# Row products behind the first squares, a split taken out of the junction chains, and deferred lows and bonus products in mixer 2, in a two-block transformer kernel on one Trainium2 core

## The reference, cut to what matters

```
for i in 0, 1:
    x += 0.5 * rms(swiglu(rms(x)))         # FFN "i0", width 2816
    x += rms(mixer_i(rms(x)))              # mixer 0: GLA and gated delta rule; mixer 1 ("mixer 2"): RWKV-7 and LRU
    x += 0.5 * rms(swiglu(rms(x)))         # FFN "i1"
```

## Time and profile before

| | us |
|---|---|
| median of 3 runs | 2829.31 (2826.69 to 2831.57) |
| profiled execution, its own time | 2830.72 |
| its span, first to last instruction | 2828.7 |
| PE busy | 2680.0 (95%) |
| weight loads / DVE / ACT busy | 2134.7 / 1558.9 / 1032.8 |
| mean granted clock of TensorE | 0.97 |

### The profile page before, as it was taken

How to read it: one execution, slowest core, us unless ns; L and a number is a source line. 1 busy time by engine, 2 the same in 40 slices (tenths; PEclk the granted TensorE clock), 3 DMA queues, 4 the chain that set the end, 5 groups by cost and what they waited for, 6 DMA issues and landing times.

```text
span 2828.7 us, 37623 instructions
## 1 busy us (share of the span) xinstructions
PE 2680.0 (95%) x15612; PEld 2134.7 (75%) x15612; DVE 1558.9 (55%) x2235; ACT 1032.8 (37%) x1536; POOL 18.8 (1%) x39
## 2 busy tenths in 40 slices
PE   7999799989999999999999999999999898999997
PEld 4766575668888788787888887888876687788886
DVE  6875867585244663634643446424465866553344
ACT  3354536442223354224422234222346422432222
POOL 0100000000000000000000000000000000000000
PEclk9999999999999997999999999999999999999998
DMA  8611231122332320112223232233222200232322
GB/s 313 233 54 64 88 115 57 55 75 88 105 98 79 100 75 30 39 31 67 90 86 108 89 98 86 89 101 102 78 90 69 65 4 3 82 97 84 110 78 72
DMA packets 71448, 243.90 MB, mean 86 GB/s; under 512 B 7920, under 2 KB 8176, under 8 KB 70256
## 3 DMA queue, kind: packets, MB, share of 16 engines
q1 hardware_dynamic: 66240, 222.11, 24.5%
q0 software_dynamic: 5040, 19.40, 1.9%
HBM read 239.38 MB, written 2.10 MB: 85 GB/s over the span
## 4 chain that ended last, share of the span: by engine, by line
PE 86%; DVE 7%; ACT 3%; issue 2%; DMA 1%; SPq 0%; DVEq 0%; ACTq 0%
PE bank L418 84%; ACT work L1471 1%; DVE work L2120 1%; DMA work<-w_ada 1%; PE bank L624 1%; DVE weights_low L2137 1%; ACT weights_high L1537 1%; DVE residual L2120 1%; DVE work L2314 1%; DVE work L2337 1%; DVE rstd L2127 0%; ACT silu_gate L1471 0%; ACT L1471 0%; ACT normed L1471 0%; DMA residual<-x_in 0%
## 5 line engine op out<-in xcount | busy, mean ns | idle before, releaser
L418 PE MATMUL bank<-normed,weights_high 128*128 128x512 f32 x4848 | 1543.0, 400 | 36.8 <-ACT normed L1471 36.8
L418 PEld LDWEIGHTS bank<-normed,weights_high 128*128 128x128 f32 x4848 | 914.8, 191 | 265.7 <-issue 80.1
L418 PE MATMUL bank<-normed,weights_low 128*128 128x512 f32 x2424 | 955.8, 394 | 0.0
L1537 ACT ACTIVATE weights_high<-ring 128x1024 fp32r<-128x1024 f32 (+2 forms) x431 | 420.7, 979 | 881.9 <-PE bank L418 881.8
L2137 DVE TENSOR_TENSOR weights_low<-ring,weights_high 128x1024 fp32r<-128x1024 f32 (+2 forms) x431 | 484.0, 1125 | 433.0 <-ACT weights_high L1537 429.5
L418 PEld LDWEIGHTS bank<-normed,weights_low 128*128 128x128 f32 x2424 | 461.8, 191 | 97.8
L418 PE MATMUL bank<-hidden,weights_high 128*128 128x512 f32 x1408 | 433.4, 389 | 0.0
L418 PEld LDWEIGHTS bank<-hidden,weights_high 128*128 128x128 f32 x1408 | 264.3, 188 | 54.8
L2510 DVE TENSOR_TENSOR silu_gate<-bank,rstd 128x512 f32<-128x512 f32 x176 | 120.8, 690 | 325.1 <-PE bank L418 325.0
L418 PE MATMUL bank<-hidden,weights_low 128*128 128x512 f32 x704 | 273.9, 389 | 0.0
L418 PE MATMUL bank<-work 64*64 64x64 f32 (+6 forms) x1600 | 146.0, 315 | 11.6 <-DVE work L2987 6.1
(11 more groups left out here) (263 smaller groups left out, 1934.3 us busy)
## 6 DMA issues: line engine op xcount, KB each, us to landing
ring<-w_k SPq DMA_DIRECT2D x303, 512.0 KB, 3.5
ring<-w_d SPq DMA_DIRECT2D x64, 384.0 KB, 3.0
ring<-w_d SPq DMA_DIRECT2D x64, 320.0 KB, 2.8
work<-w_ada POOLq DMA_DIRECT2D x32, 512.0 KB, 6.6
work<-w_shift SPq DMA_DIRECT2D x4, 1024.0 KB, 13.4
work<-w_ada SPq DMA_DIRECT2D x7, 512.0 KB, 19.1
constants<-cst_in SPq DMA_DIRECT2D x1, 2176.0 KB, 19.9
residual<-x_in SPq DMA_DIRECT2D x4, 512.0 KB, 6.2
```

What stands on the lines that cost most here:

```text
L418: return pe.matmul(o, lhsT, rhs, start=start, stop=stop, skip_group_check=True)
L1537: nc.scalar.activation(WH[:, u % SPLIT, 0:w], RING[:, u % SLOTS, 0:w], ACT.Copy).then_inc(unit_high, 1)
```

## The change

On PE, `shift_rows(0)` moves behind ms, to rows 1 to 3. At the FFN junctions `high` and `low` of the fourth next unit go behind the last output tile: `high` just ahead of the root, `low` between the reciprocal and the wait for the spread. At the mixout junctions only `low` moves, to the same place. In mixer 2 the lows of mixout's units 0 to 3 move from units 18 to 21 of the projection to the four steps of `rwkv`; bonus products move behind units 20 and 21; ly's third and fourth tile get buffers of their own (two of the running decay sums' tiles, free once `rkb` 3 is done), squares alternate between two buffers, and copies 20 and 21 no longer wait for `lru_out`. ACT makes an empty Sigmoid after unit 4's copy (`RSTD[:, 0, 8:9]`).

```diff
+        def gelu_input(i):
+            return (raw(U_LY), raw(U_LY + 1), cst("sel"), tile(12))[i]
+        def gelu_square(i):
+            return (STATE[:], tile(23))[i % 2]
@@ PE: layer_norm, odd_projection, program
                     step(mm(PS[6][:], cst("onesD"), tile(0)), "mean", norm)
-                    shift_rows(0)
-                    elif j in (19, 20):
-                        bonus(2 * j - 38)
-                        bonus(2 * j - 37)
+                    elif j in (20, 21):
+                        bonus(2 * j - 40)
+                        bonus(2 * j - 39)
-                    for i in range(1, 4):
+                    for i in range(4):
                         shift_rows(i)
@@ ACT: ffn
                         high(down + 2 * t + SPLIT)
-                        high(down + 2 * t + 1 + SPLIT)
+                        if q == 0 or t < KT - 1:
+                            high(down + 2 * t + 1 + SPLIT)
...
+                high(down + 2 * KT - 1 + SPLIT)
                 root(("post", f))
@@ ACT: odd_projection
-                        act.wait_ge(*(dve_done("gelu0", i - 1) if i else dve_done("kgated", 3)))
-                        a(STATE[:], raw(j), ACT.Square, "gelu0", i, ...)
-                        if i:
-                            gelu_gate(i - 1)
-                        else:
+                        act.wait_ge(*(dve_done("kgated", 3), dve_done("rkb", 1), dve_done("gelu0", 0), dve_done("gelu0", 1))[i])
+                        a(gelu_square(i), gelu_input(i), ACT.Square, "gelu0", i, ...)
+                        if i >= 2:
+                            gelu_gate(i - 2)
+                        elif i == 0:
...
+                    if j == U_WA:
+                        a(RSTD[:, 0, 8:9], v("one"), ACT.Sigmoid)
...
+                gelu_gate(2)
                 gelu_gate(3)
@@ DVE: post_norm, ffn
                 reciprocal_std(("post", name))
+                low(last_low)
                 dve.wait_ge(*pe_done("spread", ("post", name)))
...
                         low(down + 2 * t + SPLIT)
-                        low(down + 2 * t + 1 + SPLIT)
+                        if q == 0 or t < KT - 1:
+                            low(down + 2 * t + 1 + SPLIT)
@@ DVE: odd_projection
                     if j >= U_LY + 2:
-                        lru_out(j - 2 - U_LY)
-                        dve.wait_ge(*dve_done("ylru", j - 2 - U_LY))
+                        dve.wait_ge(*dve_done("rkb", 3))
...
-                    if j > LEAD:
+                    if LEAD < j < N_ODD - SPLIT:
                         low(u0 + j + SPLIT)
...
-                    elif j >= 19:
-                        if j == 19:
-                            queries_decayed(2)
-                            queries_decayed(3)
-                        lru_hidden(j - 19)
-                        gelu_inner(j - 19)
-                        bonus(j - 19)
-                lru_hidden(3)
-                bonus(3)
+                    elif j == 19:
+                        queries_decayed(2)
+                        queries_decayed(3)
+                    elif j >= 20:
+                        lru_hidden(j - 20)
+                        gelu_inner(j - 20)
+                        bonus(j - 20)
+                for i in (2, 3):
+                    lru_hidden(i)
+                    gelu_inner(i)
+                    bonus(i)
+                    lru_out(i - 2)
                 lru_out(2)
-                gelu_inner(3)
                 lru_out(3)
@@ DVE: rwkv, program
                 for tt in range(TT):
+                    low(UNIT0["mixout1"] + tt)
                     dve.wait_ge(*pe_done("rmat", tt, 4))
...
-                    low(UNIT0[f"mixout{i}"] + k + SPLIT)
-                post_norm(f"mix{i}", 6 * i + 3, 1.0, f"{i}1", 6 * i + 4)
+                    if k < KT - 1:
+                        low(UNIT0[f"mixout{i}"] + k + SPLIT)
+                post_norm(f"mix{i}", 6 * i + 3, 1.0, UNIT0[f"ffn{i}10"] + LEAD, f"{i}1", 6 * i + 4)
```

More of the change, by code:

```diff
@@ L1912, in gelu_gate @@
                     act.wait_ge(*dve_done("gelu0", i))
-                    a(raw(U_LY + i), raw(U_LY + i), ACT.Sigmoid, "gelu", i, scale=float(np.sqrt(8 / np.pi)), chain=False)
+                    a(gelu_input(i), gelu_input(i), ACT.Sigmoid, "gelu", i, scale=float(np.sqrt(8 / np.pi)), chain=False)
                 for j in range(N_ODD):
@@ L1923, in odd_projection @@
                         i = j - U_LY
[L1924 to L1928 removed]
+                        act.wait_ge(*(dve_done("kgated", 3), dve_done("rkb", 1), dve_done("gelu0", 0), dve_done("gelu0", 1))[i])
+                        a(gelu_square(i), gelu_input(i), ACT.Square, "gelu0", i, scale=float(np.sqrt(0.044715)), chain=False)
+                        if i >= 2:
+                            gelu_gate(i - 2)
+                        elif i == 0:
                             act.wait_ge(*dve_done("shift", U_GL))
@@ L2296, in total_of_output, with post_norm @@
                       chain=False)
-            def post_norm(name, w, factor, following=None, w2=None):
+            def post_norm(name, w, factor, last_low, following=None, w2=None):
                 reciprocal_std(("post", name))
+                low(last_low)
                 dve.wait_ge(*pe_done("spread", ("post", name)))
@@ L2844, in lru_hidden @@
                 def lru_hidden(j):
-                    x = raw(U_LY + j)
+                    x = gelu_input(j)
                     dve.wait_ge(*pe_done("bonus", j))
@@ L2849, in gelu_inner @@
                 def gelu_inner(j):
-                    x = raw(U_LY + j)
+                    x = gelu_input(j)
                     dve.wait_ge(*act_done("gelu0", j))
                     dve.wait_ge(*dve_done("lhidden", j))
-                    d(stt(x, STATE[:], 1.0, x, ALU.add, ALU.mult), "gelu0", j, chain=False)
+                    d(stt(x, gelu_square(j), 1.0, x, ALU.add, ALU.mult), "gelu0", j, chain=False)
                 def lru_out(j):
                     dve.wait_ge(*act_done("gelu", j))
-                    d(ve.tensor_tensor(GATE[:, j, :], GATE[:, j, :], raw(U_LY + j), ALU.mult), "ylru", j, chain=False)
+                    d(ve.tensor_tensor(GATE[:, j, :], GATE[:, j, :], gelu_input(j), ALU.mult), "ylru", j, chain=False)
                 def lru_gated(j):
@@ L3151, in _ @@
                 ffn(f"{i}0")
-                post_norm(f"{i}0", 6 * i + 1, 0.5, f"mix{i}", 6 * i + 2)
+                post_norm(f"{i}0", 6 * i + 1, 0.5, UNIT0[f"mix{i}"] + LEAD, f"mix{i}", 6 * i + 2)
                 pre_norm(f"mix{i}", 6 * i + 2, UNIT0[f"mix{i}"])
```

5 lines of the change are left out of this document (2 added, 3 removed).

## The result

The changed kernel takes 2804.23 us against 2828.0 us of the kernel before in the same comparison, ratio 0.9917 with the interval 0.9904 to 0.9929: 23.8 us faster. (2804.23 is the median of five executions; a sixth took 8554.87 us in a slow state and is left out, and with it the median would be 2805.03.) The forecast was 2809.0, from a gain of 20.3. The profiled execution took 2805.82 us, its span is 2804.0 us, 24.7 under the span before.

The account below looks back on a forecast made before the run. PE bounds the dense stages (86% of the span); the rest is PE waiting for chains of small steps. Start 1.8, FFN junctions 9.9, mixout junctions 1.1, mixer 2 7.5 sum to 20.3 off 2829.3: 2809.0 us, range 2802 to 2818.

Parts of the forecast that it names:

- the forecast case: Whole kernel: the moved steps leave the waiting chains as worked out, 20.3 us gained, 2809.0 us; chance 0.63.
- FFN junctions: Behind three FFNs: high and low leave the chain before the next leading units; 9.9 us net, ends 5.5 and 12.
- The gross size: Three FFN junctions: 11.3 us shorter from last product's end to spread's end, before any loss to the clock.
- The charge for the clock: Three FFN junctions: leading units run 1.0 us more at the lower level at each, costing 1.4 us in all.
- Mixout junctions: Two junctions behind mixout: low moves from between root and reciprocal to beside the spread; 1.1 us, ends 0.5 and 3.
- Start: Kernel start: without row 0's products ahead, ms ends sooner and shift() gains 1.8 us, ends 0 and 2.9.
- Sigmoid: Mixer 2: the table load leaves the chain ahead of the gates' sigmoids; 1.3 us, up to 1.5 more if clock holds.
- Tail: End of mixer 2's projection: four lows, gelu waits and closing ACT wait off DVE's path, one low added; 6.2 us.
- A: Start and five junctions: the clock takes the gain back, leaving 13 us, 2816 us; chance 0.15.
- B: Mixer 2's tail: PE or ACT becomes late for DVE, waits return, lows uncovered; gain 14 us, 2815 us; chance 0.14.
- C: Whole kernel: steps were hidden or the same waits return elsewhere; gain under 5.7 us; chance 0.05.
- D: Start and five junctions: PE stays at 1.2 GHz through the opened gap or longer; slower, 2844 us; chance 0.03.

Follow-up runs that it names:

- the halves: Kernel before with only the four lows deferred to rwkv, 2827.02 us; kernel before with only the gelu buffers and later bonus products, 2828.46 us.
- the lows alone: Kernel before with only mixout 2's four lows deferred to rwkv's steps: copy 18 to first mask 30.58 us, against 30.07 before; single run 2827.02 us.

## Why the prediction was right, and where its steps were not

**Right in sum.** 23.8 us by the medians against 20.3, inside the range, and the forecast case is the one that came: high and low off the chain at the three FFN junctions, low beside the spread at the mixout junctions, no gelu wait, PE without a gap from unit 19 to the last bonus product, lows hidden in steps 1 to 3 of `rwkv`. That the sum is so near is in part luck: by the marks the start is 2.0 us short of its term and mixer 2's stage 2.3 over, and 3.3 us of the 24.7 between the two profiles were won by no part of the change.

**FFN junctions, 9.9 forecast.** The gross size from the last FFN's chain, 11.3, was good: 11.9. The charge for the clock, 1.4, was right in size and in its reason: the leading units run at the lower level for 1.0 us more at a junction, as charged, since they start 3.7 to 4.2 us sooner and the rise comes only 2.7 to 3.4 sooner behind ms. The stage with nothing else in it gives back 0.56 of 4.23, where 0.47 was charged. The whole stretch from fall to rise became shorter by 3.4 us, but what it lost lay ahead of the leading units, under the small matmuls, and the gross size has that already. `high` costs nothing where it went; left in its old place it would have cost 0.6 to 0.8.

**Mixout junctions, 1.1 forecast:** 0.96 and 1.03 by the first leading product, 1.0 net by the two stages (0.56 and 0.45), half of it given back as forecast: the rise came 4.76 and 4.17 us behind the first leading product before, 5.65 and 5.42 in the changed kernel. No run has this part alone.

**Start, 1.8 forecast, the step that failed.** The gap of 1.5 us that opens ahead of the first square was seen, and "about 4 us" from ms's start to the rise was right on the average: 2.9 to 5.5 in the five executions, mean 4.1. Three things were off. The term was set halfway to a case in which the pace rises as before, and none of the five was that case. `mod` was put 17.1 us behind ms; in two of the five the clock fell again during the small matmuls of the columns (2.64 us instead of 1.94), which makes it 17.6. And the start in the profile of before was 0.3 us longer than the mean of seven (32.67 against 32.36). The gain measured -0.5 to 1.4, mean 0.5; only with products in the gap does the mechanism yield 2.2.

**Sigmoid, 1.3 forecast** with "up to 1.5 more" if the clock holds: it held in every profile with the Sigmoid. Alone 2.95, in the changed kernel 2.25. The 0.7 between them lies in the leading units and not at the Sigmoid: from the first leading product to the small-weight products ahead of unit 4's copy the changed kernel took 34.33 us (2069.11 to 2103.44), the kernel before 33.70, which is the junction's charge for the clock once more. The larger end should have been the estimate: the clock had fallen in a wait of 3.13 us that the step shortened.

**Tail, 6.2 forecast:** 6.5. The sum was right but its terms are no terms: four lows at 4.5 and the waits at 2.9 can't be had singly. By the traces of the halves the move of the bonus products, which the working mentions only as cover, is what turns the time off DVE's queue into time won.

**Mixer 0, no term.** Of the 6.8 us in its stage, 3.5 are the junction's. The rest is luck of the profile of before: four kernels whose code is the old one there took 383.45 to 383.72 us from FFN 00's ms to mixout 0's, the profile of before 387.01. Its clock was low for 47.8 us between that junction's leading units and mixout 0's ms, that of the four and of the changed kernel for 41.0. Two of its stretches lasted 10.2 us, with PE busy throughout:

```profile
1059.40:1069.60 10.20, 10.20 (x36) 8.94 (x36) 0.72 (x2) 0.44 (x1) 0.00 (x0) 0.51 0.00 0
1097.00:1107.20 10.20, 10.20 (x35) 7.80 (x35) 0.04 (x1) 1.28 (x3) 0.00 (x0) 0.50 0.06 22
```

(windows of the kernel before). Taken out, the two profiles differ by 21.4 us, nearer to the forecast than they look. The same luck goes the other way too: with the FFN junctions alone changed this stage took 377.20 us, with its clock low for 34.1. What decides between these levels, the runs don't show. The prediction's "all six rises in the trace came within 4.6 us of dense work" leaves out mixer 0, whose stretches of 10.2 us don't fit it, and behind mixout 0 it was 4.8.

**The rivals.** A, the clock takes it back: its half on the start came true (0.5), its half on the junctions did not, 0.9 to 1.3 us more of the leading units at the lower level at four of the five and 0.3 at the other, where it asks for 3.6. B is refuted by the whole tail, but the lows alone showed how it would have looked: a wait that moves to PE. C fell with the FFN junctions, the tail and the Sigmoid each run by itself. D never came near.

## What to carry to other kernels

Price a step off a queue by who waits for the engine and for whom it waits next: the tail's halves were worth -0.5 and 2.0 us, together 6.5. Where a dense stage follows a chain of small steps, the chain's length is one cost and the clock behind it another of about 2 us here; idle products in PE's waits, with the start's gap filled, bought the second back for 12 us, half of what all the reordering had won. And look at one stretch in several executions before a term is made of it.

## What the runs showed of the hardware that was not expected

- A PE that is never idle does not hold the upper level: in mixer 0, with 128x1 matmuls between the dense ones, the granted clock was 0.51 and 0.50 with PE busy for all of 10.20 us, and ahead of the first of the two stretches PE was busy for all of 6.90 us (1052.5 to 1059.4) at 1.00. The same instructions took 3.3 us more in that execution than in four others. With the changed FFN junctions the same stage took 380.1 to 380.3 us in four profiles and 376.7 to 379.7 in five.
- Small matmuls with gaps of 0.66 and 0.57 us between them can be enough for a fall: with them open the spread behind FFN 00 took 1.42 and 1.86 us, with one product of 128x512 in each 1.05. Whether the gaps or the small matmuls do it is not shown.
- Where the clock rises at the start varies by 2.4 us in one and the same program: 8.95 and 6.56 us behind the mean's first pass, and the leading units came 32.86 and 30.96 us behind it. The Trainium skill (TensorE: Matmul & The Clock Gate, Part 1) says that the rise hangs on where the first matmul lands, and varies by 500 ns either way. That it varies, these two executions agree, by more than the page's figure; that the landing is the reason, no run here shows.
